# Three of four down units per MLP quarter computed with seven half-block products instead of eight

## The chip, the cores and the metric

The kernel runs on one core of a Trainium2 chip. The metric is the device time of one execution in microseconds, the median of 3 runs. Before the change these are 2278.57, 2278.39 and 2278.43 us.

## The reference, cut to what matters

Two decoder layers over 512 tokens of width 1024, all float32. Each has a token mixer (retention and stick-breaking attention, not touched by the change) and an MLP with a hidden width of 4096:

```python
h2 = _modulate(_rmsnorm(x, norm_mlp_g[l]), shift2, scale2)
u = jnp.square(jax.nn.relu(h2 @ w_up[l]))          # (512, 1024) @ (1024, 4096)
x = x + gate2[:, None, :] * (u @ w_down[l])        # (512, 4096) @ (4096, 1024)
```

## The kernel before

Activations lie transposed: channels in 128 partitions, 8 tiles of 128 channels (`k`), 512 tokens in the free dimension. To keep float32 accuracy each operand is split into a high part and a low part (`h_hi`, `h_lo`; `w_hi`, `w_lo`; `y_hi`, `y_lo` for u), and a product is three matmuls: high by high, high by low, low by high. Weights come in units of 256 output columns by 1024 rows: one 1 MB DMA into `w_raw` (two buffers, s = unit mod 2), ScalarE copies to `w_hi`, GpSimd subtracts to get `w_lo`. The DMA of a unit waits until GpSimd is done with the unit two before it. Each engine's program is written out by hand, in order, with semaphores between the engines; nothing is reordered.

The MLP runs in four quarters of the hidden width (f = 0 to 3). A quarter has eight units: 0 to 3 make 1024 channels of u (two tiles each), 4 to 7 multiply them by the down weights and add into x (`x_T`). In this text "unit 5" is the second down unit of a quarter.

A plain unit is `half_unit` twice: 8 tiles by 3 matmuls into one PSUM bank of 512 columns, so 48 matmuls of 512 columns. The up units of quarters 1 to 3 are made otherwise (`up_seven`): the unit is seen as a 2 by 2 block product (even and odd input tiles, first and second 128 output columns, first and second 256 tokens) and computed with seven half-block products instead of eight, a Winograd form. Each half-block product is 4 tiles by 3 matmuls of 256 columns: 84 matmuls of 256 columns for a unit. TensorE issues products one, five, four of the unit before, six, three, two, seven (L1513 is the matmul in `half_product`). The form needs sums of weight blocks (`sums_31`, `sums_24`: VectorE L2138, L2141, L2144 in `sum_weights`, then splits on ScalarE L586 to L593, low parts on GpSimd and on VectorE L2151) and sums of h blocks (t1 to t4: VectorE in `sum_h` and `sum_t`, once in each layer, in the down units of quarter 0). The extra copies of the weight sums, `wx_hi` and `wx_lo`, have two buffers. PSUM banks are joined by VectorE with the help of ScalarE copies (`first_copied`, `fifth_copied`, `sixth_copied`), since VectorE adds a PSUM bank and an SBUF copy of another. All products of ScalarE that TensorE waits for in a seven-product unit are in one in-order queue: high parts of the next unit's weights, the copies, the relu.

In quarter 0 the up units are plain: ScalarE takes the relu out of PSUM (L1014), VectorE squares (L2215), ScalarE makes `y_hi` (L1017), VectorE `y_lo` (L2218), for each of the eight tiles; then unit 4 waits for these tiles one after another (`u_split`). Unit m of a quarter sets its bank free with the relu.

Of the kernel before, what the change touches and what calls it, by code (L numbers as in the profile page):

```python
# [9 lines left out]
P = 128  # L10
D = 1024
SEQ = 512
# [74 lines left out]
FIRST_SEVEN = 1  # L87
SEVENS = 4 * (QUARTERS - FIRST_SEVEN)
PAIRS = KT // 2
T1, T2, T3, T4 = range(4)  # L90


def seven(layer, f, m):

    return SEVENS * layer + 4 * (f - FIRST_SEVEN) + m


def is_seven(unit):
    return unit >= MLP and (unit - MLP) % 8 < 4 and (unit - MLP) // 8 >= FIRST_SEVEN

# [36 lines left out]
def hybrid_trunk(nc, x, c, norm_mix_g, w_in, w_ret_out, w_sb_out, w_mix_out, norm_mlp_g,  # L137
# [7 lines left out]
    with ctx:  # L145
# [32 lines left out]
        wx_hi = nc.alloc_sbuf_tensor_at("wx_hi", [P, 2, 3, PAIRS, P], f32r, offset=work_base + 4 * 6144)  # L178
        wx_lo = nc.alloc_sbuf_tensor_at("wx_lo", [P, 2, 3, PAIRS, P], f32r, offset=ya_base)
# [68 lines left out]
        sums_31 = slab[:, 4 * PAIRS * HALF:4 * PAIRS * HALF + 2 * PAIRS * P].rearrange("p (a i n) -> p a i n", a=2, i=PAIRS)  # L248
        fifth = relu_t[:, 1, 0:HALF]
# [109 lines left out]
        h_summed, t_made, t_half, t_ready = sem("h_summed"), sem("t_made"), sem("t_half"), sem("t_ready")  # L359
# [98 lines left out]
        def _(pool):  # L458
# [23 lines left out]
            def seven_low(layer, unit):  # L482

                s, f, m = unit % 2, *divmod(unit - MLP, 8)
                q = seven(layer, f, m)
# [6 lines left out]
                for k in range(0, KT, 4):  # L492
                    ins = pool.tensor_tensor(w_lo[:, 2 * s + 1, k:k + 4:2, :], sums_31[:, 0, k // 2:k // 2 + 2, :],
                                             w_hi[:, 2 * s + 1, k:k + 4:2, :], ALU.subtract)
                ins.then_inc(seven_lo, 1)
                pool.wait_ge(seven_hi, 5 * q + 3)
                for i in range(0, PAIRS, 2):
                    ins = pool.tensor_tensor(wx_lo[:, s, 0, i:i + 2, :], sums_31[:, 1, i:i + 2, :],
                                             wx_hi[:, s, 0, i:i + 2, :], ALU.subtract)
                ins.then_inc(seven_lo, 1)  # L500
                pool.wait_ge(seven_hi, 5 * q + 5)
# [22 lines left out]
        def _(act):  # L524
# [51 lines left out]
            def seven_split(pair, unit, which):  # L576

                s, slot = unit % 2, 2 * (unit % 2)
                f, m = divmod((2 * pair + unit) % LAYER_UNITS - MLP, 8)
                q = seven((2 * pair + unit) // LAYER_UNITS, f, m)  # L580
                if which == 0:
                    act.wait_ge(raw_in[s], 16 * (pair + unit // 2 + 1))
                    ins = act.activation(w_hi[:, slot, :, :], w_raw[:, s, :, 0:P], ACT.Copy)  # L583
                elif which == 1:
                    act.wait_ge(sums_made, 3 * q + 1)
                    ins = act.activation(w_hi[:, slot + 1, 0:KT:2, :], sums_31[:, 0, :, :], ACT.Copy)  # L586
                elif which == 2:
# [141 lines left out]
            for layer in range(DEPTH):  # L729
# [1559 lines left out]
```

## Time and profile before

| | |
|---|---|
| median of 3 runs | 2278.43 us |
| profiled execution | 2278.35 us |
| its span (first to last instruction) | 2276.6 us |
| TensorE busy | 2256.1 us (99%) |
| VectorE, ScalarE, GpSimd busy | 1246.6, 976.2, 1228.2 us |
| granted TensorE clock, mean | 1.00 |

The chain that ended last is TensorE in 97% of the span. One MLP layer takes the stretch from about 806 to 1149 us in layer 0, and the same 1116.3 us later in layer 1. In a timeline row a first number is the start, the second how long the row's instructions took together; the bracket at the end is idle time of the engine before it and what ended it.

### The profile page before, as it was taken

The page shows a single profiled execution, that of the slowest core. Times are in us where ns is not written, and L with a number is a line of the kernel's source. Part 1 is how long each engine was busy: PE and PEld are TensorE (multiplying, and loading weights), DVE is VectorE, ACT ScalarE, POOL GpSimd, SP SyncE. Part 2 cuts the span into 40 slices and gives each one's busy share as a digit, 9 for nine tenths or more (in the row PEclk, how much of TensorE's full clock was granted, in tenths as well). Part 3 has the DMA queues.
Part 4 walks back from the last instruction along what each step waited for, and adds up shares of the span by engine and source line. Part 5 has one row for each costly group of instructions (what it writes and reads, how often), then busy time and mean ns, then how long its engine had stood idle before and what let it go on. Part 6 is the DMA issues. An engine that isn't in the chain of part 4 may idle for free.

```text
span 2276.6 us, 30866 instructions
## 1 busy us (share of the span) xinstructions
PE 2256.1 (99%) x12424; PEld 1921.7 (84%) x12424; DVE 1246.6 (55%) x1695; ACT 976.2 (43%) x1291; POOL 1228.2 (54%) x1538
## 2 busy tenths in 40 slices
PE   7999999999999999999999999999999999999998
PEld 5888888888888888998988888888888789898997
DVE  5776668546653346454476757441666524463453
ACT  4332233256675254453433323232666834353442
POOL 4454554544454457666555455455444444676663
PEclk9999999999999999999999999999999999999999
DMA  9445444422222222333334444222222222332332
GB/s 305 136 153 161 158 134 148 130 75 74 75 83 84 93 93 92 105 101 93 121 125 152 159 141 142 79 93 93 74 75 75 74 93 75 111 93 93 112 93 74
DMA packets 242094, 252.67 MB, mean 111 GB/s; under 512 B 3984, under 2 KB 237600, under 8 KB 241952
## 3 DMA queue, kind: packets, MB, share of 16 engines
q1 hardware_dynamic: 240272, 247.00, 33.6%
q10 hardware_dynamic: 1680, 3.70, 0.5%
q8 instruction: 98, 1.61, 0.3%
q14 instruction: 44, 0.36, 0.0%
HBM read 248.59 MB, written 2.10 MB: 110 GB/s over the span
## 4 chain that ended last, share of the span: by engine, by line
PE 97%; DVE 1%; ACT 1%; DMA 0%; issue 0%; SPq 0%; DVEq 0%; ACTq 0%
PE proj L1190 54%; PE att L1513 11%; PE proj L1213 6%; PE proj L1247 4%; PE proj L1230 4%; PE att L1230 4%; PE att L1403 2%; PE att L1453 2%; PE att L1278 2%; PE proj L1278 2%; PE att L1463 1%; PE att L1441 1%; PE att L1385 1%; PE proj L1352 1%; PE att L1416 1%; PE proj L1118 1%
## 5 line engine op out<-in xcount | busy, mean ns | idle before, releaser
L518 POOL TENSOR_TENSOR w_lo<-w_raw,w_hi 128x256 fp32r<-128x256 f32 x1280 | 1027.4, 836 | 934.7 <-ACT w_hi L564 797.1
L564 ACT ACTIVATE w_hi<-w_raw 128x1024 fp32r<-128x1024 f32 (+1 forms) x300 | 304.0, 1021 | 319.1 <-PE proj L1190 182.7
L1190 PE MATMUL proj<-h_hi,w_hi 128*128 128x512 f32 x1024 | 405.5, 396 | 0.0
L1190 PE MATMUL proj<-h_hi,w_lo 128*128 128x512 f32 x1024 | 399.3, 390 | 0.0
L1190 PE MATMUL proj<-h_lo,w_hi 128*128 128x512 f32 x1024 | 398.8, 389 | 0.0
L1190 PE MATMUL proj<-y_hi,w_hi 128*128 128x512 f32 x784 | 305.1, 389 | 0.0
L1190 PE MATMUL proj<-y_lo,w_hi 128*128 128x512 f32 x784 | 305.1, 389 | 0.0
L1190 PE MATMUL proj<-y_hi,w_lo 128*128 128x512 f32 x784 | 305.0, 389 | 0.0
L1190 PEld LDWEIGHTS proj<-h_hi,w_lo 128*128 128x128 f32 x1024 | 192.2, 188 | 41.2
L1190 PEld LDWEIGHTS proj<-h_hi,w_hi 128*128 128x128 f32 x1024 | 192.3, 188 | 40.4 <-issue 1.6
L1190 PEld LDWEIGHTS proj<-h_lo,w_hi 128*128 128x128 f32 x1024 | 192.6, 188 | 37.6
L1649 DVE SCALAR_TENSOR_TENSOR slab<-slab,c_act 128x256 f32<-128x256 f32 x280 | 177.0, 632 | 9.9
L1190 PEld LDWEIGHTS proj<-y_hi,w_lo 128*128 128x128 f32 x784 | 147.2, 188 | 30.7
L1190 PEld LDWEIGHTS proj<-y_hi,w_hi 128*128 128x128 f32 x784 | 147.2, 188 | 30.3
L1190 PEld LDWEIGHTS proj<-y_lo,w_hi 128*128 128x128 f32 x784 | 147.2, 188 | 29.9
L1767 DVE SCALAR_TENSOR_TENSOR x_T<-proj,mod,x_T 128x512 f32<-128x512 f32 x66 | 49.5, 750 | 196.1 <-PE proj L1190 196.1
L573 ACT ACTIVATE w_hi<-w_raw 128x512 fp32r<-128x512 f32 x64 | 37.0, 625 | 199.7 <-PE proj L1230 130.9
L488 POOL TENSOR_TENSOR w_lo<-w_raw,w_hi 128x256 fp32r<-128x256 f32 x96 | 90.3, 971 | 58.2 <-ACT w_hi L583 58.2
L2013 DVE TENSOR_TENSOR_SCAN slab<-slab,work 128x1280 f32<-128x1280 f32 x32 | 91.4, 2858 | 1.1
L2011 DVE SCALAR_TENSOR_TENSOR work<-att,work 128x1280 f32<-128x1280 f32 x32 | 47.6, 1487 | 60.9 <-ACT work L845 60.9
L2021 DVE TENSOR_TENSOR work<-att,slab 128x1280 f32<-128x1280 f32 x32 | 47.7, 1492 | 51.4 <-PE att L1453 51.4
L1247 PE MATMUL proj<-w_hi,h_hi 128*128 128x256 f32 x256 | 73.1, 286 | 0.0
(341 smaller groups left out, 4754.2 us busy)
## 6 DMA issues: line engine op xcount, KB each, us to landing
w_raw<-in_w_in SPq DMA_DIRECT2D x88, 1024.0 KB, 5.1
slab<-in_w_ada SPq DMA_DIRECT2D x42, 1024.0 KB, 6.3
w_raw<-in_w_up SPq DMA_DIRECT2D x32, 1024.0 KB, 5.6
w_raw<-in_w_down SPq DMA_DIRECT2D x32, 1024.0 KB, 5.2
w_raw<-in_w_ret_out SPq DMA_DIRECT2D x16, 1024.0 KB, 5.1
w_raw<-in_w_sb_out SPq DMA_DIRECT2D x8, 1024.0 KB, 5.1
w_raw<-in_w_mix_out SPq DMA_DIRECT2D x8, 1024.0 KB, 5.1
ya<-in_x SPq DMA_DIRECT2D x1, 2048.0 KB, 8.2
```

The source lines that it names most:

```text
L488: ins = pool.tensor_tensor(w_lo[:, 2 * s, k:k + 2, :], w_raw[:, s, k:k + 2, 0:P], w_hi[:, 2 * s, k:k + 2, :], ALU.subtract)
L518: ins = pool.tensor_tensor(w_lo[:, slot, k:k + 2, :], w_raw[:, s, k:k + 2, P * j:P * (j + 1)], w_hi[:, slot, k:k + 2, :], ALU.subtract)
L564: ins = act.activation(w_hi[:, 2 * s + j, ks, :], w_raw[:, s, ks, P * j:P * (j + 1)], ACT.Copy)
L1190: last = pe.matmul(proj[:, j, :], w[:, slot, k, :], a[:, k, :], start=k == 0 and n == 0, stop=k == KT - 1 and n == 2)
L1213: last = pe.matmul(first_bank if j == 0 and first_bank is not None else proj[:, j, :], w[:, slot, k, :], a[:, k, :], start=k == 0 and n == ...
L1230: last = pe.matmul(v_of(t).rearrange("p (a n) -> p a n", a=4), a[:, k, t * P:(t + 1) * P], w[:, :, k, :], start=k == 0 and n == 0, stop=k ...
L1247: last = pe.matmul(proj[:, t // 2, UNIT * (t % 2):UNIT * (t % 2 + 1)].rearrange("p (a n) -> p a n", a=2), a[:, k, t * P:(t + 1) * P], w[:, ...
L1278: last = pe.matmul(dst, w[:, slot, k, :], a[:, k, HALVES[t]], start=k == 0 and i == 0, stop=k == KT - 1 and i == 2)
L1513: last = pe.matmul(bank, w[b][at(i)], rows[a](i), start=begins and i == j == 0, stop=ends and i == PAIRS - 1 and j == 2, skip_group_check= ...
L1649: ins = dve.scalar_tensor_tensor(acc, raw[:, k, :], c_act[:, k:k + 1], acc, ALU.mult, ALU.add)
L1767: free(dve.scalar_tensor_tensor(x_T[:, k, :], proj[:, half, :], mod[:, ds(gate_col + k, 1)], x_T[:, k, :], ALU.mult, ALU.add), half)
L2013: own.link(dve.tensor_tensor_scan(logits[:, a, ::-1], carry_t[:, ::-1], terms[:, a, ::-1], 0.0, ALU.mult, ALU.add))
```

## The change

Units 5, 6 and 7 of quarters 0, 1 and 2 are made with seven half-block products too, in both layers: 18 units. Unit 4 of each quarter, and all down units of quarter 3, stay plain. What comes with it:

- Four sums of u blocks (`tu_sum`, `sum_tu`), made for each pair of tiles as soon as it is there: four VectorE instructions of 128x256 for each up unit of quarters 0 to 2. In quarters 1 and 2 ScalarE copies one half tile out of PSUM first (`b12_copied`). Then four splits of 128x1024 on ScalarE (`split_tu`) and four on VectorE (`low_tu`) for each quarter, in unit 4.
- The sums of h (`sum_t`) are no longer made from a float32 sum of h in `ya`, but from `h_hi` and `h_lo`: ten VectorE instructions of 128x1024 instead of eight. They stand in up units 1 and 2 of quarter 0 instead of down units 4 and 5.
- The weight sums take one buffer (`wx_hi`, `wx_lo` without the dimension of 2). One sum is made in place in `w_raw`, one in `decay_t`: four VectorE instructions of 128x512 instead of one of 128x1024 and two of 128x512. The split of sums two and four (`seven_split(..., 3)`) and `low_sums` wait until product three of the unit before is done.
- Down units made of seven products add to x from the joined banks (`add_tile`).

```diff
-FIRST_SEVEN = 1
-SEVENS = 4 * (QUARTERS - FIRST_SEVEN)
+DOWN = 4
+SEVEN_UNITS = ([8 * f + m for f in range(1, QUARTERS) for m in range(DOWN)]
+               + [8 * f + DOWN + d for f in range(QUARTERS - 1) for d in (1, 2, 3)])
...
-        wx_hi = nc.alloc_sbuf_tensor_at("wx_hi", [P, 2, 3, PAIRS, P], f32r, offset=work_base + 4 * 6144)
-        wx_lo = nc.alloc_sbuf_tensor_at("wx_lo", [P, 2, 3, PAIRS, P], f32r, offset=ya_base)
+        wx_hi, wx_lo = (nc.alloc_sbuf_tensor_at(name, [P, 3, PAIRS, P], f32r, offset=ya_base + 4 * 3 * PAIRS * P * i)
+                        for i, name in enumerate(("wx_hi", "wx_lo")))
...
```

ScalarE in each unit made of seven products (`ahead` splits the next unit's weights), then at the entry to the down units of quarters 0 to 2:

```diff
                     ahead(0)
+                    if after_up:
+                        high_u(f, 2 * j - 2)
                     act.wait_ge(made[1], q + 1)
                     act.activation(relu_t[:, 0, 0:HALF], chain_bank(q), ACT.Copy).then_inc(first_copied, 1)
                     ahead(1)
                     act.wait_ge(made[5], q + 1)
                     act.activation(fifth, FIFTH, ACT.Copy).then_inc(fifth_copied, 1)
                     ahead(2)
...
-                    ahead(3)
                     ahead(4)
...
+                    act.wait_ge(made[3], q + 1)
+                    ahead(3)
...
+                    for which in (1, 2, 4):
+                        seven_split(layer, f, DOWN + 1, which)
+                    split_tu(f, T1)
+                    split_tu(f, T2)
+                    seven_split(layer, f, DOWN + 1, 3)
+                    split_tu(f, T3)
+                    split_tu(f, T4)
...
```

TensorE's waits and products, the t sums of h on VectorE, and VectorE's down units:

```diff
+                    wait_t(f, j, T1)
                     pe.wait_ge(seven_lo, 3 * q + 3)
...
                     pe.wait_ge(fifth_copied, q + 1)
-                    half_product(3, wx, in_extra(s, 2), h_block(1, 1), FIFTH, False, True)
+                    half_product(3, wx, in_extra(2), block_of(up, 1, 1), FIFTH, False, True)
...
+                    if which in (T1, T3):
+                        b, a = ((b12, b11), (b22, b12))[which // 2]
+                        own.link(dve.tensor_tensor(t[which], b[0], a[0], ALU.subtract))
+                        own.link(dve.tensor_tensor(t[which], t[which], b[1], ALU.add))
+                        ins = dve.tensor_tensor(t[which], t[which], a[1], ALU.subtract)
...
+                def down(pair, f):
+                    if f > 0:
+                        square_first(f, 3)
+                        join_22(seven(layer, f, 3))
+                    sum_weights_13(f, DOWN + 1)
+                    if f > 0:
+                        first_of_u(f, 3)
+                        square_second(f, 3)
+                        second_of_u(f, 3)
+                    sum_weights_24(f, DOWN + 1)
+                    low_tu(f, T1)
+                    low_tu(f, T2)
+                    add_to_x(pair, MLP + DOWN, 0, 0, gates + KT * GATE2)
+                    low_sums(f, DOWN + 1)
+                    low_tu(f, T3)
+                    low_tu(f, T4)
+                    add_to_x(pair, MLP + DOWN, 1, 1, gates + KT * GATE2)
+                    for d in (1, 2, 3):
+                        seven_unit(f, DOWN + d)
```

VectorE's order in up units 1 and 2 of quarter 0. Before, from tile 2 on (L2215 squares a tile, L2218 makes its low part):

```order
L2215 TENSOR_TENSOR work<-work 128x512 [waits bank_free0]
L2218 TENSOR_TENSOR y_lo<-work,y_hi 128x512 [waits u_half]
L2215 TENSOR_TENSOR work<-work 128x512 [waits bank_free1]
L2218 TENSOR_TENSOR y_lo<-work,y_hi 128x512 [waits u_half]
L2215 TENSOR_TENSOR work<-work 128x512 [waits bank_free0]
L2218 TENSOR_TENSOR y_lo<-work,y_hi 128x512 [waits u_half]
```

The same place after the change (L2346 and L2350 square and make the low part, L2187 to L2189 and L2193, L2194 are t sums of h, L2249 sums of u):

```order
L2346 TENSOR_TENSOR work<-work 128x512 [waits tu_made,bank_free0]
L2350 TENSOR_TENSOR y_lo<-work,y_hi 128x512 [waits u_half]
L2187 TENSOR_TENSOR work<-h_hi 128x1024
L2188 TENSOR_TENSOR work<-work,h_lo 128x1024 [waits dve_own]
L2189 TENSOR_TENSOR work<-work,h_lo 128x1024 [waits dve_own]
L2346 TENSOR_TENSOR work<-work 128x512 [waits bank_free1]
L2350 TENSOR_TENSOR y_lo<-work,y_hi 128x512 [waits u_half]
L2249 TENSOR_TENSOR work<-work 128x256
L2249 TENSOR_TENSOR work<-work 128x256 [waits tu_made]
L2249 TENSOR_TENSOR work<-work 128x256
L2249 TENSOR_TENSOR ya<-work 128x256 [waits tu_made]
L2193 TENSOR_TENSOR work<-h_hi,work 128x1024 [waits t_made]
```

Two pairs of a square and its low part that followed each other now have up to seven instructions between them.

VectorE after the change in unit 4 of quarter 0, from the weight sums of unit 5 to the first weight sum of unit 6 (L2209, into `decay_t`); L2255 is `low_tu`, L1843 adds the halves of unit 4 to x, L2226 is `low_sums`:

```order
L2209 TENSOR_TENSOR decay_t<-w_raw 128x512 [waits raw_in1]
L2210 TENSOR_TENSOR w_raw<-w_raw 128x4x128
L2217 TENSOR_TENSOR att<-w_raw 128x512 [waits sums_made]
L2220 TENSOR_TENSOR att<-w_raw,att 128x512 [waits sums_made]
L2255 TENSOR_TENSOR tu_lo_63<-work,h_hi 128x1024 [waits tu_half]
L2255 TENSOR_TENSOR tu_lo_64<-work,h_lo 128x1024 [waits tu_half]
L1843 SCALAR_TENSOR_TENSOR x_T<-proj,mod,x_T 128x512 [waits proj_done]
L2226 TENSOR_TENSOR wx_lo<-att,wx_hi 128x1024 [waits seven_hi]
L2255 TENSOR_TENSOR tu_lo_65<-work,tu_hi_61 128x1024 [waits tu_half]
L2255 TENSOR_TENSOR tu_lo_66<-ya,tu_hi_62 128x1024 [waits tu_half]
L1843 SCALAR_TENSOR_TENSOR x_T<-proj,mod,x_T 128x512 [waits proj_done]
L2209 TENSOR_TENSOR decay_t<-w_raw 128x512 [waits seven_lo,raw_in0]
```

The first weight sum of unit 6 is the last of twelve.

ScalarE after the change from the entry of unit 5 in quarter 0 (L598: first high part of unit 6, L1002 copies product one, L601 splits the sum in `decay_t`, L1007 copies product five for the join):

```order
L598 ACTIVATE w_hi<-w_raw 128x1024 [waits raw_in0,proj_done]
L1002 ACTIVATE work<-att 128x256 [waits made1]
L601 ACTIVATE w_hi<-decay_t 128x4x128 [waits sums_made]
L1007 ACTIVATE ada_rows<-att 128x256 [waits made5]
L604 ACTIVATE wx_hi<-w_raw 128x512 [waits sums_made]
```

The copy of product five stands behind the split of that weight sum, here as in the up units before the change.

## Rows read from the trace of the kernel before

**Rows 1.** The page: busy time (share of span), and the chain that ended last by engine.

```profile
PE 2256.1 (99%) x12424; PEld 1921.7 (84%) x12424; DVE 1246.6 (55%) x1695; ACT 976.2 (43%) x1291; POOL 1228.2 (54%) x1538
...
PE 97%; DVE 1%; ACT 1%; DMA 0%; issue 0%; SPq 0%; DVEq 0%; ACTq 0%
```

**Rows 2.** The chain in order of time (start, us, what): layer 0, quarters 0 to 2.

```profile
820.54 76.19 PE proj L1190 x336
896.72 38.87 PE att L1513 x324
938.46 42.19 PE proj L1190 x186
980.65 38.87 PE att L1513 x324
```

**Rows 3.** Stretches of quarter 0's up units, then quarter 1's up and down units: busy time.

```profile
core 0: us, PE busy (x) PEld busy (x) DVE busy (x) ACT busy (x) POOL busy (x), PEclk, DMA share, GB/s
820.00:857.90 37.90, 37.90 (x171) 31.45 (x170) 12.48 (x16) 16.72 (x23) 22.77 (x31) 1.00 0.35 112
...
896.60:938.40 41.80, 41.80 (x344) 41.41 (x343) 27.16 (x39) 25.58 (x44) 30.91 (x39) 1.00 0.34 109
938.40:980.60 42.20, 42.20 (x188) 34.93 (x187) 10.81 (x13) 10.04 (x12) 24.55 (x34) 1.00 0.34 102
```

**Rows 4.** VectorE's timeline, quarter 0: tiles 1 to 4 (start us, us).

```profile
822.60 0.85 DVE L2215 TENSOR_TENSOR work<-work 128x512 f32<-128x512 f32 x1 [0.74 <-ACT work L1014]
824.14 1.15 DVE L2218 TENSOR_TENSOR y_lo<-work,y_hi 128x512 fp32r<-128x512 f32 x1 [0.70 <-ACT y_hi L1017]
826.67 1.15 DVE L2215 TENSOR_TENSOR work<-work 128x512 f32<-128x512 f32 x1 [1.38 <-ACT work L1014]
828.52 1.15 DVE L2218 TENSOR_TENSOR y_lo<-work,y_hi 128x512 fp32r<-128x512 f32 x1 [0.70 <-ACT y_hi L1017]
...
838.94 0.69 DVE L2218 TENSOR_TENSOR y_lo<-work,y_hi 128x512 fp32r<-128x512 f32 x1 [0.70 <-ACT y_hi L1017]
```

**Rows 5.** GpSimd's timeline, the same stretch.

```profile
822.16 6.97 POOL L518 TENSOR_TENSOR w_lo<-w_raw,w_hi 128x256 fp32r<-128x256 f32 x8 [2.63 <-ACT w_hi L564]
```

**Rows 6.** VectorE's timeline, unit 6 of quarter 0: t sums, alone and beside GpSimd.

```profile
870.23 1.22 DVE L2115 TENSOR_TENSOR work<-ya 128x1024 f32<-128x1024 f32 x1
871.48 1.64 DVE L2118 TENSOR_TENSOR work<-ya,work 128x1024 f32<-128x1024 f32 x1
```

**Rows 7.** GpSimd's timeline, the same stretch and the next: eight instructions of one form.

```profile
870.75 4.36 POOL L518 TENSOR_TENSOR w_lo<-w_raw,w_hi 128x256 fp32r<-128x256 f32 x4 [1.08 <-ACT w_hi L564]
...
881.95 2.83 POOL L488 TENSOR_TENSOR w_lo<-w_raw,w_hi 128x256 fp32r<-128x256 f32 x4
```

**Rows 8.** VectorE by line and shape: count, busy us, mean ns of one.

```profile
L2174 DVE TENSOR_TENSOR att<-work,att 128x256 f32<-128x256 f32 x24 | 10.1, 422 | 0.0
...
L1802 DVE TENSOR_TENSOR work<-work 128x256 f32<-128x256 f32 x18 | 8.4, 466 | 0.0
L2151 DVE TENSOR_TENSOR wx_lo<-att,wx_hi 128x1024 fp32r<-128x1024 f32 x6 | 7.4, 1226 | 8.1 <-ACT wx_hi L591 8.1
```

**Rows 9.** ScalarE by line and shape.

```profile
L983 ACT ACTIVATE work<-att 128x256 f32<-128x256 f32 x24 | 9.2, 384 | 8.8 <-PE att L1513 8.0
...
L943 ACT ACTIVATE t_hi<-work 128x1024 fp32r<-128x1024 f32 x8 | 8.0, 1044 | 0.0
```

**Rows 10.** VectorE's timeline, from the last up unit into unit 4 of quarter 1.

```profile
935.62 0.70 DVE L2162 TENSOR_TENSOR att<-work,att 128x512 f32<-128x512 f32 x1 [0.67 <-ACT work L997]
936.23 0.42 DVE L2174 TENSOR_TENSOR att<-work,att 128x256 f32<-128x256 f32 x1
...
939.13 0.70 DVE L2167 SCALAR_TENSOR_TENSOR att<-work,att 128x512 f32<-128x512 f32 x1 [1.46 <-ACT work L955]
940.49 0.69 DVE L2157 TENSOR_TENSOR y_lo<-att,y_hi 128x512 fp32r<-128x512 f32 x1 [0.67 <-ACT y_hi L949]
942.61 0.75 DVE L1767 SCALAR_TENSOR_TENSOR x_T<-proj,mod,x_T 128x512 f32<-128x512 f32 x1 [1.42 <-PE proj L1190]
```

**Rows 11.** ScalarE's timeline, first up unit of quarter 1.

```profile
898.19 0.38 ACT L978 ACTIVATE work<-att 128x256 f32<-128x256 f32 x1 [0.37 <-PE att L1513]
```

More of the change, by code:

```diff
@@ L482, in seven_low @@
             def seven_low(layer, unit):
[L484 to L485 removed]
+                s = unit % 2
+                q = seven(layer, *divmod(unit - MLP, 8))
+                second = raw_block(s)[:, A21, :, :]
                 pool.wait_ge(seven_hi, 5 * q + 1)
@@ L1017, in up @@
                             act.activation(y_hi[:, k, :], u_t[:, half, :], ACT.Copy).then_inc(u_half, 1)
-                            split_weights(pair, MLP + m + 2, half)
-                def down(pair, f, last):
-                    for m in range(4 if not last else 2 if layer < DEPTH - 1 else 3):
+                            if m < 3:
+                                split_weights(pair, MLP + m + 2, half)
+                            if m >= 2:
+                                split_t(2 * (m - 2) + half)
@@ new lines, in last_down @@
+                def last_down(pair, f):
+                    q = seven(layer, f, DOWN - 1)
+                    high_u(f, KT - 2)
+                    act.wait_ge(made[7], q + 1)
+                    split_weights(pair, MLP + DOWN + 1, 0)
+                    relu_second(q)
+                    high_u(f, KT - 1)
+                    split_weights(pair, MLP + DOWN + 1, 1)
+                    if layer < DEPTH - 1:
+                        products(pair, MLP + DOWN, 0)
+                        act.dma_start(rope_t, rope).then_inc(rope_in, 16)
+                    for m in range(2 if layer < DEPTH - 1 else 3):
@@ L2219, in quarter @@
                                               ALU.subtract).then_inc(u_split, 1)
-                    for m in range(4 if not last else 2 if layer < DEPTH - 1 else 3):
+                            if half == 1:
+                                for which in range(4):
+                                    sum_tu(0, m, which, u_t[:, 0, :], u_t[:, 1, :])
+                            if m in (1, 2):
+                                sum_t(2 * (m - 1) + half)
+                            elif k == 6:
+                                low_t(T1)
@@ L2225, in quarter @@
-                            add_to_x(pair, MLP + 4 + m, half, k, gates + KT * GATE2)
-                            if f == FIRST_SEVEN - 1:
-                                for i in ((0, 1), (2, 3))[half] if m == 0 else ():
-                                    sum_h(i)
-                                for which in ((T1, T2), (T3, T4))[half] if m == 1 else ():
-                                    sum_t(which)
-                            if not last and k == 3:
-                                sum_weights(pair + 4, f + 1, 0)
@@ L2233, in quarter @@
-                            if not last and k == 5:
-                                low_sums(f + 1, 0)
-                            if f == FIRST_SEVEN - 1 and k in (5, 6):
-                                for which in ((T1, T2), (T3, T4))[k - 5]:
-                                    low_t(which)
-                            if last and layer < DEPTH - 1:
+                            add_square(2 * layer + 2, k - 1, at_layer)
+                            add_to_x(pair, MLP + DOWN + m, half, k, gates + KT * GATE2)
```

441 lines of the change are left out of this document (266 added, 175 removed).

## The prediction

> **What bounds the kernel now.** I read the page's busy times and chain first: TensorE is busy for 99% of the span and is 97% of the chain that ended last [rows 1]. Only fewer or cheaper matmuls, or a wait of TensorE, can change the time. The chain in order of time then shows how tight this is in the stretch that changes: 336 plain matmuls in 76.19 us, 324 of the short ones in 38.87 us, and plain ones again, without a hole [rows 2]. The stretches show what the others have left: VectorE is busy for 12.48 of 37.9 us in the up units of quarter 0, for 27.16 of 41.8 us in up units of seven products, for 10.81 of 42.2 us in down units; GpSimd is at 22.77, 30.91 and 24.55 us [rows 3]. The timelines of single instructions come last, for the orders in which these two could become late.
>
> **The matmuls removed.** A plain one takes 76.19/336 = 226.8 ns, a unit of 48 takes 10.88 us. A short one takes 38.87/324 = 120.0 ns, a unit of 84 takes 10.08 us [rows 2]. Each converted unit saves 0.80 us, not an eighth of 10.88, because 256 columns cost more than half of 512. 18 units: 14.5 us less.
>
> The Trainium skill (TensorE: Matmul & The Clock Gate, "Back-to-back issue gap") gives columns/2.4 + 2.5 ns, which is 215.8 and 109.2 ns; as an estimate by that page a unit would save 1.19 us, 18 units 21.4 us. The rows have 226.8 and 120.0 ns, and the sum goes by them.
>
> **Quarter 0, up units: VectorE.** Unit 4 should start at 820.54 + 3 x 10.88 = 853.2 and asks for tile 7 of u 21 matmuls later, at 857.95. VectorE now does more between the tiles. After tile 1, ready at about 825.3 [rows 4], and until tile 7's low part is made it has: six tiles, each a square and a low part of 0.69 us with a gap of 0.70 us while ScalarE makes the high part [rows 4], 6 x 2.08 = 12.5 us; three sets of four sums of u, 0.42 to 0.47 us each [rows 8], less the 0.1 by which instructions without a wait overlap, 3 x 1.65 = 4.95; ten t sums of 1.22 us [rows 6], 12.1; one low part of t, 1.2. That is 30.7 us, so tile 7 is ready at 856.0, 1.9 us early. This is the lower bound, with no extra.
>
> The extra is in the rows. A VectorE instruction with two SBUF inputs that begins while GpSimd runs takes longer: 1.15 instead of 0.69 us [rows 4], 1.64 instead of 1.22 [rows 6], so 0.42 to 0.46 us for each, whatever its length. GpSimd loses time too: four instructions take 4.36 instead of 2.83 us beside two of 1.22 [rows 7], eight take 6.97 instead of 5.66 beside four of 0.69 [rows 5]. The Trainium skill (GPSIMD Engine Reference, "1. Specifications") states that GpSimd's SBUF interfaces are shared with VectorE and contended by VectorE instructions with two SBUF inputs. This speaks against the change, since nearly all that it adds in quarter 0 has two; the trace agrees with it: `low_sums` has a PSUM input and stays at 1.226 us [rows 8].
>
> In this stretch GpSimd has about 20 instructions, the rest of unit 2's low parts and those of units 3 and 4. Each can lengthen one VectorE instruction: at most 20 x 0.46 = 9.2 us. Six fall into VectorE's gaps, and some beside instructions that follow without a wait. I take 12, 5.5 us: tile 7 at 861.5, between 856.0 and 865.2. TensorE stands still for about 3.5 us.
>
> **Quarter 0, entry to unit 5.** In the new order the first weight sum of unit 6 is the last of twelve VectorE instructions, ScalarE's split of it stands ahead of the copy of product five, and product three needs that copy. Due for product three: 864.07 + 36 x 0.12 = 868.4. From tile 7's low part on VectorE has: sums of u 1.55, weight sums of unit 5 0.69 x 4 = 2.65, 0.65 of waiting for ScalarE's splits, two low parts 2.35, an add 0.65 (0.75 less the overlap) [rows 10], `low_sums` 1.2, two low parts 2.35, an add 0.7, the weight sum 0.65: 12.75. ScalarE's split and the copy of 0.384 [rows 9] add 1.05: 13.8 us. Queued behind the split on ScalarE is only that copy, and TensorE waits for it. Lower bound: 856.0 + 13.8 = 869.8, 1.4 us late. With four or five extras of 0.46, of which the wait for ScalarE swallows some, 15.4 us: 861.5 + 15.4 = 876.9, 8.5 us late. This contains the 3.5 us. Upper bound: 865.2 + 15.6 = 880.8, 12.4 us late. ScalarE's four new splits of 1.04 us [rows 9] lie beside this. Value taken: 8.5 for each layer, 17.0 us.
>
> **Quarters 1 and 2, up units.** Four sums of u with a PSUM input (0.42 us, no extra) and one copy of 0.38 us on ScalarE are added for each unit; weight sums cost 2.8 to 3.6 instead of 3.05 us. VectorE goes from 8.3 to between 9.7 and 10.6 us in a unit of 10.08 us. Only units 1 and 2 of a quarter carry all of it, so it falls behind by 1 us at most and recovers in unit 3. The tightest user is product four, which needs the join made 1.8 us after a unit's start and begins at 2.88. I take nothing; the other end is 0.3 us for a quarter.
>
> **Quarters 1 and 2, entry to unit 5.** The same twelve instructions. From the start of unit 4 (935.5 in quarter 1): the join ends at 1.15 and the second square starts at 3.65 as now, the gap behind it is 0.67 and the low part ends at 5.7 [rows 10]; three sums of u to 6.7, two weight sums to 8.1, the remaining seven instructions 2.35 + 0.65 + 1.2 + 2.35 + 0.65 + 0.65 = 7.85, and 0.45 for one extra: 16.4. Split and copy: 17.25. Product three is due at 12.32 + 4.32 = 16.64, since unit 4 with the guest product four takes 10.88 + 1.44. Late by 0.6 us, with three more extras 2.0; I take 1.4. Four such entries: 5.6 us. ScalarE's wait for the end of product one (0.37 us idle) is not on this path [rows 11].
>
> **At nothing.** The wait of the single buffer: after product three's end 2.9 us of other products are left in the unit and 4.3 more come before product six of the next, and a split of 1.04 and `low_sums` of 1.23 us [rows 8, 9] fit. If they didn't, product six would wait. `add_tile` replaces `add_to_x` one for one. GpSimd does ten instructions in a unit instead of a plain one's eight, 1.4 us more, and has 4 us free in it. The up units of quarter 3 change only names of buffers. The DMA of a unit is triggered by GpSimd's last low part, 9 us or more ahead of its use.
>
> **The sum.** -14.5 + 17.0 + 5.6 = +8.1 us. On the profiled execution's 2278.35 us (span 2276.6 and 1.75 around it, 0.08 under the median of the runs) that is 2286.5, and on the median's scale too.
>
> **Rivals.** First: VectorE and GpSimd rarely meet. The lower bounds then hold: -14.5 + 2 x 1.4 + 4 x 0.6 = -9.3, 2269.1 us. For it: GpSimd is idle for 40% of the up stretch [rows 3]. Against: its next work is started by ScalarE right behind the high part, when VectorE starts on the sums.
>
> Second, which also covers the change doing no more than its matmul count says: nothing waits, TensorE alone counts: 2263.9 us. For it: VectorE's total in a quarter stays under TensorE's. Against: the order of single instructions above.
>
> Third: GpSimd falls behind too. It is slowed 1.53 us by two instructions of 1.22 us [rows 7]; in unit 5 of quarter 0 it starts 5 us late and has the low parts of t and u beside it, so product five of units 5 and 6 waits for `seven_lo`. It decides when these low parts come over 2 us later than VectorE's chain above allows, and costs 2 us in each layer behind a quarter 0 at its upper bound: -14.5 + 2 x 14.4 + 4 x 2.0 = +22.3, 2300.7 us. For it: the rates in [rows 5, 7]. Against: a unit of seven products has over 3 us of slack on GpSimd in [rows 3].
>
> **Chances.** Forecast 0.55, first rival 0.15, second 0.13, third 0.15, others 0.02. What a measurement here can tell from no change is 0.2%, 4.6 us. The forecast's own range is 2278 to 2294; about a third of it lies under 2283. Faster: 0.13 and most of the first rival, 0.28. Same: 0.20. Slower: 0.52. The range of 8 in 10 takes the first rival and leaves out half of the second and half of the third: 2266 to 2297.
>
> **What would show it.** In the profile after: 120 ns for the down units' short matmuls; in quarter 0 a hole of TensorE inside the first half of unit 4, released by VectorE's L2350, and a second before product three of unit 5, released by ScalarE's copy L1007; in quarters 1 and 2 only the second, of 0.6 to 2 us. VectorE at its limit between 825 and 861 us, with t sums of 1.6 us. I am wrong if TensorE runs through these places, if holes come at other products (a release by GpSimd means the third rival), or if the short matmuls with `tu` operands take another time.

## The result, and the profile of the changed kernel

The changed kernel took 2307.65 us (median of 4 runs, 2306.34 to 2307.76) against 2278.41 us (2278.17 to 2278.57) for the kernel before, run beside it: a ratio of 1.0127, 95% interval 1.0110 to 1.0145. It is slower by 29.2 us. The forecast was 2286.5 us, range 2266 to 2297; the direction was right, the size was not. The profiled execution took 2307.67 us, with a span of 2305.8.

Its page, to be held against [rows 1]: busy time, and the chain that ended last by engine.

```profile
PE 2258.9 (98%) x13072; PEld 1952.0 (85%) x13072; DVE 1451.5 (63%) x1987; ACT 1057.2 (46%) x1439; POOL 1302.7 (56%) x1574
...
PE 89%; DVE 7%; ACT 2%; issue 1%; DMA 0%; SPq 0%; DVEq 0%; ACTq 0%
```

There are 648 matmuls more, as meant: 1512 of half the columns (18 x 84) stand in the place of 864. But VectorE is now 7% of the chain, and TensorE's busy time has risen by 2.8 us although it has less to do. The waits of TensorE, longest first (us in total, times, longest), name the places in the MLP; none of these rows stands in the profile before.

```profile
PE att L1556 <- ACT ada_rows L1007: 14.9, 6, 3.0
PE proj L1233 <- DVE y_lo L2350: 8.2, 4, 2.2
...
PE proj L1233 <- issue: 2.5, 2, 1.3
...
PE proj L1233 <- ACT work L1035: 0.8, 2, 0.4
```

The first row is the forecast's wait before product three of unit 5, the second its wait inside unit 4 of quarter 0. The other two stand at the start of unit 4 and one unit before it. The four rows make 26.4 us, and -14.5 + 26.4 is +11.9, not +29.2. The chain in order of time (start, us, what) shows where the others are. The first three rows are quarters 0 to 2 of layer 0, the last three those of layer 1:

```profile
880.98 67.69 PE att L1556 x540
...
967.67 66.56 PE att L1556 x540
...
1053.25 66.53 PE att L1556 x540
...
2013.71 66.39 PE att L1556 x540
...
2099.11 65.07 PE att L1556 x540
...
2183.19 66.55 PE att L1556 x540
```

All six rows are the same 540 short matmuls, without a wait, from product three of unit 5 to the end of the next up units. One takes 65.07 us, which is 120.5 ns each; the others take 1.3 to 2.6 us more, 8.4 us in all. The stretches behind the waits tell why (busy times by engine, then the granted clock in the third column from the end; first quarter 0 of layer 0, then quarters 1 and 2 of layer 1):

```profile
864.00:866.00 2.00, 1.47 (x4) 1.18 (x5) 1.97 (x6) 1.64 (x2) 0.28 (x1) 0.50 0.00 0
866.00:868.00 2.00, 2.00 (x6) 1.61 (x5) 2.00 (x2) 0.63 (x1) 2.00 (x3) 0.50 0.00 0
...
870.00:872.00 2.00, 2.00 (x10) 1.62 (x10) 1.71 (x3) 2.00 (x3) 2.00 (x2) 1.00 0.00 0
...
882.00:884.00 2.00, 2.00 (x11) 2.00 (x11) 1.97 (x3) 0.64 (x3) 2.00 (x3) 0.50 0.03 8
...
2098.00:2100.00 2.00, 0.89 (x7) 0.90 (x8) 1.97 (x3) 1.61 (x4) 1.85 (x3) 1.00 0.00 0
2100.00:2102.00 2.00, 2.00 (x19) 2.00 (x18) 1.11 (x2) 1.48 (x3) 2.00 (x3) 1.00 0.00 0
...
...
2185.00:2187.00 2.00, 2.00 (x11) 2.00 (x10) 0.23 (x1) 1.02 (x1) 2.00 (x4) 0.50 0.00 0
```

Behind a wait TensorE is busy all the time, but a row of 2 us counts 6 matmuls of 512 columns where the row at full clock counts 10, and 11 short ones where it counts 19. The granted clock is 0.50, its lower level of 1.2 GHz; before the change it was 1.00 in every stretch of [rows 3]. The starts of single matmuls give the price: 427 ns apart at 512 columns (866.40 and 866.83 below) instead of 226.8, 213 ns at 256 columns instead of 120.

```profile
861.40 0.50 PE L1233 MATMUL proj<-y_hi,w_hi 128*128 128x512 f32 x1 [1.92 <-DVE y_lo L2350]
...
864.53 0.80 PE L1233 MATMUL proj<-y_hi,w_hi 128*128 128x512 f32 x1 [2.15 <-DVE y_lo L2350]
...
866.40 0.63 PE L1233 MATMUL proj<-y_lo,w_hi 128*128 128x512 f32 x1
866.83 0.63 PE L1233 MATMUL proj<-y_hi,w_lo 128*128 128x512 f32 x1
...
880.98 0.58 PE L1556 MATMUL att<-y_hi,wx_hi 128*128 128x256 f32 x1 [3.01 <-ACT ada_rows L1007]
```

From 865.12 to 869.82 eleven matmuls lose 2.2 us in this way, and 2.4 us are lost at the same place of layer 1. With the 8.4 us above, TensorE loses 13.0 us at the low clock. That makes up the difference: measured from start to start, each of the 14 stops takes 0.2 to 0.5 us more than the idle time listed for it (the matmul at 864.53 is followed by the next one 0.59 us later), 4.2 us in all, and -14.5 + 26.4 + 13.0 + 4.2 = +29.1 us.

The Trainium skill (TensorE: Matmul & The Clock Gate, "What's actually happening") says that low is the clock's resting state and that activity of the engine releases it; the trace agrees as far as every slow stretch here follows a wait, but the equal wait at 2099.11 has none behind it.

Not all of the 13.0 us lengthen the kernel. VectorE works from tile 7 to the late weight sum without once waiting for TensorE, and product three comes 16.5 us after tile 7, whether unit 4 ran at the low clock or not (864.47 to 880.98 here; 858.05 to 874.57 in the experiment e7, where unit 4 ran at full clock). At full clock TensorE would only have waited longer before product three. So the 2.2 and 2.4 us inside unit 4 cost nothing in the end, and the 8.4 us behind product three do.

VectorE's timeline in the up units of quarter 0, against the 1.22 us of [rows 6] and the 0.69 of [rows 4] (start us, us):

```profile
846.26 1.22 DVE L2187 TENSOR_TENSOR work<-h_hi 128x1024 f32<-128x1024 f32 x1
847.51 1.64 DVE L2188 TENSOR_TENSOR work<-work,h_lo 128x1024 f32<-128x1024 f32 x1
...
850.75 1.22 DVE L2346 TENSOR_TENSOR work<-work 128x512 f32<-128x512 f32 x1
852.67 0.69 DVE L2350 TENSOR_TENSOR y_lo<-work,y_hi 128x512 fp32r<-128x512 f32 x1 [0.70 <-ACT y_hi L1038]
853.28 2.26 DVE L2249 TENSOR_TENSOR work<-work 128x256 f32<-128x256 f32 x3
855.46 0.95 DVE L2249 TENSOR_TENSOR ya<-work 128x256 f32<-128x256 f32 x1
...
863.78 0.69 DVE L2350 TENSOR_TENSOR y_lo<-work,y_hi 128x512 fp32r<-128x512 f32 x1 [0.70 <-ACT y_hi L1038]
```

While GpSimd runs (from 846.65 for 5.93 us, and from 853.67), one instruction after the other takes 0.42 to 0.54 us more: the square 1.22 instead of 0.69, a sum of u 0.95 (at 855.46) instead of 0.42. The first of the three sums in the row of 2.26 us began before GpSimd did and took 0.42 us, the other two took 0.94 us each. Tile 7's low part ends at 864.47. ScalarE's timeline shows a cost that the forecast had not seen:

```profile
852.01 0.63 ACT L1038 ACTIVATE y_hi<-work 128x512 fp32r<-128x512 f32 x1 [4.02 <-DVE work L2346]
852.55 1.04 ACT L580 ACTIVATE w_hi<-w_raw 128x1024 fp32r<-128x1024 f32 x1
853.50 1.04 ACT L959 ACTIVATE t_hi<-work 128x1024 fp32r<-128x1024 f32 x1
854.44 0.58 ACT L1035 ACTIVATE work<-proj 128x512 f32<-128x512 f32 x1
```

The relu L1035 empties the bank that TensorE needs for unit 4. It stands in ScalarE's queue behind two splits and behind L1038, which had waited 4.0 us for VectorE's square. It ends at 855.02, and unit 4 starts at 855.12, after 1.3 us without a releaser in the profile ("issue").

### The profile page after: what moved, and what is told of

The parts are those of the page before. It is cut to its first block, busy times and chain, and to the rows that moved or that the text cites. A ratio compares the mean times of both kernels' runs of the same rounds, so it can differ in the third digit from the quotient of the medians.

```text
span 2305.8 us, 32925 instructions
## 1 busy us (share of the span) xinstructions
PE 2258.9 (98%) x13072; PEld 1952.0 (85%) x13072; DVE 1451.5 (63%) x1987; ACT 1057.2 (46%) x1439; POOL 1302.7 (56%) x1574
## 4 chain that ended last, share of the span: by engine, by line
PE 89%; DVE 7%; ACT 2%; issue 1%; DMA 0%; SPq 0%; DVEq 0%; ACTq 0%
PE proj L1233 40%; PE att L1556 18%; PE proj L1256 5%; PE proj L1290 4%; PE att L1273 4%; PE proj L1273 4%; PE att L1446 2%; DVE tu_lo L2255 2%; PE att L1496 2%; PE att L1321 1%; PE proj L1321 1%; PE att L1506 1%; PE att L1484 1%; PE att L1428 1%; DVE work L2249 1%
## 5 line engine op out<-in xcount | busy, mean ns | idle before, releaser
L534 POOL TENSOR_TENSOR w_lo<-w_raw,w_hi 128x256 fp32r<-128x256 f32 x1136 | 921.3, 845 | 871.7 <-ACT w_hi L580 734.1
L580 ACT ACTIVATE w_hi<-w_raw 128x1024 fp32r<-128x1024 f32 (+1 forms) x264 | 265.9, 1016 | 228.7 <-PE proj L1233 103.9
L503 POOL TENSOR_TENSOR w_lo<-w_raw,w_hi 128x256 fp32r<-128x256 f32 x168 | 174.6, 1069 | 89.7 <-ACT w_hi L598 89.7
L1233 PE MATMUL proj<-y_hi,w_hi 128*128 128x512 f32 x496 | 196.0, 395 | 10.7 <-DVE y_lo L2350 8.2
L1233 PE MATMUL proj<-y_lo,w_hi 128*128 128x512 f32 x496 | 195.1, 393 | 0.0
L1233 PE MATMUL proj<-y_hi,w_lo 128*128 128x512 f32 x496 | 194.9, 393 | 0.0
L1233 PEld LDWEIGHTS proj<-y_hi,w_hi 128*128 128x128 f32 x496 | 94.5, 190 | 32.4 <-DVE y_lo L2350 9.9
L1233 PEld LDWEIGHTS proj<-y_hi,w_lo 128*128 128x128 f32 x496 | 94.3, 190 | 20.0
L1233 PEld LDWEIGHTS proj<-y_lo,w_hi 128*128 128x128 f32 x496 | 94.5, 190 | 19.2
L824 ACT ACTIVATE work<-proj 128x512 f32<-128x512 f32 x32 | 19.1, 598 | 122.4 <-PE proj L1233 122.4
```

Of the source, the lines that this page charges most:

```text
L503: ins = pool.tensor_tensor(w_lo[:, 2 * s, k:k + 2, :], w_raw[:, s, k:k + 2, 0:P], w_hi[:, 2 * s, k:k + 2, :], ALU.subtract)
L534: ins = pool.tensor_tensor(w_lo[:, slot, k:k + 2, :], w_raw[:, s, k:k + 2, P * j:P * (j + 1)], w_hi[:, slot, k:k + 2, :], ALU.subtract)
L580: ins = act.activation(w_hi[:, 2 * s + j, ks, :], w_raw[:, s, ks, P * j:P * (j + 1)], ACT.Copy)
L1233: last = pe.matmul(proj[:, j, :], w[:, slot, k, :], a[:, k, :], start=k == 0 and n == 0, stop=k == KT - 1 and n == 2)
```

## The experiments

**e3_holes: the price of a hole by itself.** The kernel before, with a wait of its own length in each quarter.

```
HOLE = (1, 2, 4, 5, 6, 7, 9, 14)
...
 products(pair, MLP + 4 + m, half)
+if m == 1 and half == 0:
+    for _ in range(HOLE[4 * layer + f]):
+        own.link(act.activation(hole_t[:, :], upto[:, :], ACT.Copy))
+    act.sem_inc(hole, 1)
...
+if m == half == 1:
+    pe.wait_ge(hole, 4 * layer + f + 1)
```

> The kernel before, with a hole made on purpose: in unit 5 of each quarter TensorE waits before its second half until ScalarE, released by the end of the first half, has done n small copies, n = 1, 2, 4, 5 in layer 0 and 6, 7, 9, 14 in layer 1. Estimate 0.35 us a copy and 0.35 for the way there and back: holes of 0.7, 1.05, 1.75, 2.1, 2.45, 2.8, 3.5 and 5.25 us, 19.6 us in all. Theory A (behind a hole of about 2 us or more the granted clock goes to 0.5 for some 5 us, which costs about 2.4 us more): 2278.4 + 19.6 + 4 or 5 x 2.4 = 2308 to 2310 us, and the short holes cost only themselves. Theory B (a hole costs itself alone): 2298 us.

Measured: 2304.28 us (2 runs), 25.9 more. The holes were 0.44, 0.79, 1.47, 1.81, 2.15, 2.49, 3.17 and 4.88 us long, 17.2 in all. Behind the three longest TensorE was slow, for 1.7, 1.7 and 2.2 us more than at full clock; behind the fifth it was not. Its stretches behind the fifth, and around the sixth:

```profile
1995.00:1997.00 2.00, 2.00 (x11) 1.63 (x10) 0.00 (x0) 0.00 (x0) 2.00 (x4) 1.00 0.68 239
2080.00:2082.00 2.00, 1.89 (x6) 1.52 (x7) 0.00 (x0) 1.07 (x2) 0.68 (x1) 0.69 0.57 201
2082.00:2084.00 2.00, 2.00 (x6) 1.55 (x5) 0.00 (x0) 0.00 (x0) 2.00 (x4) 0.50 0.00 0
2084.00:2086.00 2.00, 2.00 (x10) 1.65 (x9) 0.00 (x0) 0.00 (x0) 0.12 (x1) 0.96 0.04 8
```

Theory A holds with a smaller size than its 2308 to 2310: the holes were shorter than estimated, and only three slow stretches came. By theory B the holes as measured would give 2295.6 us. Without any part of the change, holes make the clock fall.

**e10_equal_holes: the same length eight times.** As e3, with `HOLE = (5,) * 8`.

> e3 with five small copies at all eight places: eight holes of 2.15 us, about the length of the waits of 2.21 us that were followed by the lower clock at three places of four. In e3 one of 2.15 us was not, one of 2.49 us was. Theory A (near this length it is open whether the clock falls, so the same wait costs 2.2 us or about 4): 2278.4 + 8 x 2.1 = 2295 us and 1.2 to 2.2 us more for each place where it falls, 2297 to 2308 us, with some places of each kind in the profile. Rival (there is a fixed length between 2.15 and 2.21 us): 2295 us and no lower clock.

Measured: 2299.41 us (2 runs), 21.0 more. The waits were 1.81 us (I had read 2.15 from e3's fifth hole; five copies are its fourth), 14.5 us in all. Behind three of the eight the clock fell, and 1.6 to 1.7 us were lost at each. Around the first and behind the third:

```profile
872.00:874.00 2.00, 2.00 (x6) 1.61 (x5) 0.88 (x1) 0.65 (x1) 1.27 (x2) 0.50 0.97 315
...
1047.00:1049.00 2.00, 2.00 (x10) 1.62 (x10) 0.00 (x0) 0.89 (x1) 1.03 (x2) 1.00 0.76 267
```

So the same wait after the same work costs 1.8 or 3.5 us, and the rival, a fixed length between 2.15 and 2.21 us, is gone: 1.81 can be enough, 2.21 can be too little.

**e2_filled: the holes before product three filled with matmuls.**

```
 pe.wait_ge(first_copied, q + 1)
+if j == DOWN + 1:
+    for _ in range(2):
+        repeated(6 if f == 0 else 5, wx, in_extra(1), t_block(up, T2), chain_bank(q))
 half_product(6, wx, in_extra(1), t_block(up, T2), chain_bank(q), False, False)
```

> Before product six of unit 5 TensorE repeats its matmuls into the same sum, 24 times in quarter 0 and 20 in quarters 1 and 2 (2.9 and 2.4 us at 120 ns), so the sum of that product is another one. TensorE is then busy where it stood still, and product three starts at the same time. Theory A (a hole makes the granted clock fall, and this costs about 12 us behind the six holes before product three): 2307.7 - 12 = 2295 us, between 2292 and 2299. Theory B (the low clock doesn't hang on the holes): 2307 to 2309 us.

Measured: 2299.80 us (4 runs), 7.9 less than the changed kernel, with 128 more matmuls. The waits before product three are 0.4 us in all, and no stretch behind them is slow. The filling costs 128 x 0.12 = 15.4 us and takes away 14.5 us of waiting, with 1.4 us of new waits, so 7.9 + 0.9 + 1.4 = 10.2 us of low clock came back: the 8.4 us of the chain's rows, and 1.6 us that the stretches behind unit 4 happened to be shorter. The 12 us of the expectation were too many; theory A holds, at 2300 instead of 2295 and just outside its 2292 to 2299.

**e1_copy_first: another order on ScalarE.**

```
-ahead(1)
+if j != DOWN + 1:
+    ahead(1)
 act.wait_ge(made[5], q + 1)
 ...
 act.activation(fifth, FIFTH, ACT.Copy).then_inc(fifth_copied, 1)
+if j == DOWN + 1:
+    ahead(1)
```

> In unit 5 of quarters 0 to 2 ScalarE copies product five before it splits the first weight sum of unit 6, so product three no longer waits for twelve VectorE instructions. Theory A (the loss is made of two things: holes of TensorE, 14.9 us of them before product three, and the stretch at the lower granted clock behind each of them, about 12 us in all): both go, 2307.7 - 14.9 - 12 = 2281 us, with the holes inside unit 4 of quarter 0 left (8.2 us and their low clock). Theory B (only waits cost; the lower clock comes with the change whatever waits there are): 2307.7 - 14.9 = 2293 us, with the low stretches still there. Theory C (VectorE is behind as a whole, so the wait only moves to the next product that needs it): 2300 us or more, with holes of the same sum before products six or one of unit 6.

Measured: 2294.63 us (2292.92 to 2297.27), ratio 1.0073 [1.0056, 1.0090]. The number is near theory B's, but B is wrong: in quarters 1 and 2 no stretch is slow any more. A is wrong too in its size, because half of the wait moved:

```profile
PE proj L1236 <- DVE y_lo L2353: 8.2, 4, 2.2
PE att L1559 <- ACT work L1020: 7.8, 6, 2.0
...
PE att L1559 <- POOL wx_lo L513: 2.0, 2, 1.2
```

ScalarE's copy for product seven (L1020) is now behind three splits of late sums. This is C's mechanism in part: the sums are late, and the order on ScalarE only decides who waits.

**e4_quarter0_plain and e5_plain0_copy: quarter 0 without the change.** e4 leaves the down units of quarter 0 plain and makes the t sums of h in them; e5 adds e1's edit.

```
-SEVEN_UNITS = (... + [8 * f + DOWN + d for f in range(QUARTERS - 1) for d in (1, 2, 3)])
+SEVEN_UNITS = (... + [8 * f + DOWN + d for f in range(1, QUARTERS - 1) for d in (1, 2, 3)])
```

> The down units of quarter 0 stay plain, as in the kernel before, and the sums of h are made in them (ten VectorE instructions); only those of quarters 1 and 2 are of seven products (12 units instead of 18). Theory A (each place pays for itself): saved 12 x 0.80 = 9.6 us; lost in each of four entries to unit 5 2.4 us of waiting and up to 2 us of low clock, 9.6 to 17.6 us: 2278.4 to 2286 us, and quarter 0 costs the changed kernel the other 21 to 29 us. Theory B (the loss comes from the new form of the unit wherever it stands): two thirds of the loss stay, 2297 us.

> Quarter 0 plain (as in e4) and the copy of product five ahead of the split (as in e1). In e1 the waits of 2.2 us in quarters 1 and 2 became waits of 1.1 us before product seven, released by ScalarE's copy L1020, which now stands behind three splits of sums that VectorE makes late; no lower clock showed behind them. Theory A (the late weight sums of unit 6 decide, the order on ScalarE only shifts who feels them): e4's 2283.0 - 4 x 1.1 of waiting - 5.3 of low clock = 2273.3 us, 2272 to 2275. Theory B (the lower clock comes with the change): 2278.5 us.

Measured: e4 2283.01 us (10 runs, 2278.74 to 2284.79), ratio 1.0018 [1.0008, 1.0027]; e5 2274.22 us (10 runs), ratio 0.9982 [0.9972, 0.9992]. So quarter 0 costs the changed kernel 24.6 us, net of what its six units save. In e4 each of the four entries waits 2.2 us, with the clock low behind three of them in the profiled execution; its runs lie up to 6 us apart, and their mean granted clock goes with it, from 0.999 in the two fastest to 0.996 or 0.997 in the others: how many waits are followed by the low clock differs. In e5 they are 1.1 us and nothing is slow. A's sum of 2273.3 holds.

**e6_sums_early and e11_sums_early_alone: the weight sums of unit 6 earlier on VectorE.** e6 is e5 with this edit, e11 is e4 with it.

```
 low_tu(f, T3)
+sum_weights_13(f, DOWN + 2)
+sum_weights_24(f, DOWN + 2)
 low_tu(f, T4)
 add_to_x(pair, MLP + DOWN, 1, 1, gates + KT * GATE2)
...
-if before_seven:
+if before_seven and j != DOWN + 1:
```

> As e5, and VectorE makes the four weight sums of unit 6 ahead of the fourth low part of the sums of u and of the second addition to x, instead of behind them: nothing that ScalarE's copies of unit 5 stand behind comes late any more. Theory A: no wait of TensorE over 0.3 us in the MLP, 2278.4 - 12 x 0.80 = 2268.8 us, with 0.3 us for each of the changes between plain and seven products 2268 to 2271. Rival C (VectorE is short of time, not badly ordered): the wait moves to product four or to product seven, which need the low parts T4 and T3: 2272 us or more.

> Quarter 0 plain, the weight sums of unit 6 made early, but ScalarE's copy of product five still behind the split (e6 without e1's edit). Theory A (lateness of the sums is the cause, and ScalarE's order hurts only when they are late): 2269 to 2270 us, as e6. Rival (the split itself, 0.6 us, stands in the way of the copy): a wait of 0.3 to 0.6 us before product three at four places, 2270.5 to 2272 us.

Measured: e6 2269.29 us (2269.12 to 2269.61), ratio 0.9960 [0.9944, 0.9976]; e11 2269.44 us, the same. They beat the kernel before by 9.1 and 9.0 us, of 12 x 0.80 = 9.6 possible. e6's chain in order of time, for quarter 0, the up units of quarter 1, unit 4, and units 5 to 7 with the next up units:

```profile
820.59 76.19 PE proj L1249 x336
896.77 38.89 PE att L1572 x324
938.61 9.55 PE proj L1249 x42
948.15 69.30 PE att L1572 x576
```

No hole is left, 69.30/576 is 120.3 ns, and the pair-by-pair sums, the single buffer and `add_tile` cost nothing that can be seen. VectorE is busy for 35.38 of 42 us from 948 to 990: it was not short of time there, it was badly ordered by 2.2 us. With the sums in time ScalarE's order doesn't matter.

**e9_all18_sums_early: the same order with all 18 units.** e1's edit and e6's on the changed kernel.

> All 18 down units of seven products, as in the changed kernel, with both edits of e6 (copy of product five first, weight sums of unit 6 ahead of the low part T4). Theory A: quarters 1 and 2 run without a wait; in quarter 0 the waits of unit 4 (4.1 us) and at its start (1.3 and 0.4 us) stay with about 2 us of low clock, and VectorE, about 8 us behind by then, makes TensorE wait 2 to 4 us more in unit 5 or 6. e6's 2269.3 - 6 x 0.80 + 2 x (5.8 + 2 + 2 to 4) = 2284 to 2288 us. Theory B (quarter 0 also heals by the order): 2278 us or less.

Measured: 2291.08 us, ratio 1.0056 [1.0041, 1.0071]. Quarters 1 and 2 run without a wait, as expected. Quarter 0 doesn't heal, and is worse than the 2284 to 2288 expected: beside unit 4's waits (8.1, 2.5 and 0.8 us) there are 5.5 us in three waits released by GpSimd's L513, at product five of units 5 and 6, and the clock is low behind three waits in the profiled execution (864.57, 1986.54 and 2008.06 us), but not behind the one of 2.30 us at 886.05.

```profile
PE proj L1236 <- DVE y_lo L2353: 8.1, 4, 2.2
...
PE att L1559 <- POOL wx_lo L513: 5.5, 3, 2.4
```

**e7_thin_gpsimd and e8_short_t: why VectorE is late in quarter 0.** e7 takes GpSimd's work away beside it, e8 six of the ten instructions of the t sums. Each leaves the rest of the changed kernel as it is.

```
e7: -for k in range(ks.start, ks.stop, 2):
    +for k in range(ks.start, ks.start + 2 if MLP + 2 <= unit <= MLP + 4 else ks.stop, 2):
e8: -own.link(dve.tensor_tensor(t[which], b[0], a[0], ALU.subtract))
    -own.link(dve.tensor_tensor(t[which], t[which], b[1], ALU.add))
    -ins = dve.tensor_tensor(t[which], t[which], a[1], ALU.subtract)
    +ins = dve.tensor_tensor(t[which], b[0], a[0], ALU.subtract)
    ...
```

> The changed kernel, where GpSimd makes only a quarter of the low parts (one instruction of four) for units 2, 3 and 4 of quarter 0, so that VectorE has it hardly beside it in the up units; the other low parts are left as they were, and the output is another one. Theory A (VectorE falls behind there because nearly each of its instructions with two SBUF inputs takes 0.42 to 0.54 us more beside GpSimd): tile 7's low part comes at 857 to 858 instead of 864.5 us, the waits of unit 4 and at its start (5.7 us a layer) shrink under 1.5, product three of unit 5 starts at about 874 instead of 881.0: 2307.7 - 2 x 7 - 2 x 2.3 of low clock = 2289 us. Theory B (VectorE has simply too many instructions, GpSimd matters little): 2303 us or more.

> The changed kernel with each of the four t sums made by a single VectorE instruction (the low terms of h left out; 4 instructions instead of 10 in each layer). It takes six instructions of 1.22 to 1.75 us, 9 us, from VectorE between tiles 1 and 7. Theory A: tile 7 comes at its time, the waits in unit 4 and at its start go, product three of unit 5 stays 4 to 6 us late, since the chain from tile 7 to it (16.5 us) stays: 2307.7 - 2 x 7.5 - 2 x 2.3 = 2288 us. Rival (the waits in unit 4 come from the sums of u or from ScalarE's order): 2300 us or more.

Measured: e7 2293.38 us, e8 2291.34 us; 2289 and 2288 were expected. In both the waits of unit 4 and at its start are gone. VectorE's timeline in e7, up to tile 7's low part, without an extra:

```profile
855.97 0.69 DVE L2346 TENSOR_TENSOR work<-work 128x512 f32<-128x512 f32 x1
857.36 0.69 DVE L2350 TENSOR_TENSOR y_lo<-work,y_hi 128x512 fp32r<-128x512 f32 x1 [0.70 <-ACT y_hi L1038]
```

Tile 7 is ready at 858.05 instead of 864.47 us, with the same VectorE instructions, and the quarter itself starts 0.9 us later in this execution (its first matmul at 821.27, not 820.36): 7.3 us are GpSimd's doing. Product three starts at 874.57 instead of 880.98, again 7.3 us earlier in its quarter. In front of it a new wait of 2.0 us stands in both layers at product five, in layer 0 released by GpSimd's L513: with VectorE in time for unit 4, GpSimd is late next. But this wait is not the 3 to 4 us by which both expectations missed, because the copy of product five (L1007) is still held up by the split of the late weight sum. ScalarE in e7:

```profile
873.62 0.63 ACT L601 ACTIVATE w_hi<-decay_t 128x512 fp32r<-128x512 f32 x1 [4.70 <-DVE decay_t L2209]
874.15 0.36 ACT L1007 ACTIVATE ada_rows<-att 128x256 f32<-128x256 f32 x1
```

What was wrong is the expectations' 2 x 2.3 us of low clock inside unit 4: those lie ahead of product three and shorten only the wait there. Without them e7's sum is 2307.7 - 2 x 7.3 = 2293.1 us, and 2293.4 was measured; e8, where product three moved by the same 7.3 us, lies 1.8 us lower, with runs from 2289.6 to 2293.2.

## Why the prediction was wrong

**The matmuls removed: right.** 0.80 us a unit; e6 has 9.1 of 12 x 0.80.

**Quarter 0, up units: right in place and cause, too small.** The chain without extras (30.7 us, tile 7 at 856.0) is confirmed by e7: 858.05, or 857.1 with the later start of that execution taken off, where a quarter of GpSimd's work is left. I then took 12 extras of 0.46. In the trace 19 instructions between tile 1 and tile 7 are longer, by 9.4 us in all, and tile 7 comes at 864.5, near the upper bound of 865.2. The step that failed is "some beside instructions that follow without a wait" as a ground to count fewer: instructions issued back to back pay the extra each, so one GpSimd instruction doesn't lengthen only one. The four sums behind tile 5 are an example: the first took 0.42 us, the other three 0.94 to 0.95 each. The Trainium skill (SBUF — State Buffer, "SBUF: two separate sides") calls the pair of ports an exclusive lock held for a whole instruction, which would let each of them wait anew; the equal size of the extras at 256 and 1024 elements agrees with it. The sharing goes both ways: beside VectorE GpSimd took 2.42 us for two instructions and 5.93 for four, against 2.83 for four in [rows 7].

**A queue that I did not follow.** I priced the wait for tile 7 (3.5 us) and not what stands behind ScalarE's high part: the relu that frees the bank. It makes 0.4 and 1.3 us more of waiting in each layer. Like the low clock inside unit 4 these lie ahead of product three, and only shorten the wait there.

**Quarter 0, entry to unit 5: right in place, order and releaser, too small.** Product three came at 880.98, not 876.9; due was 868.4. From tile 7 it took 16.5 us, not 15.4. It was 12.6 us late, not 8.5: 3.0 us of the difference come from tile 7, 1.1 us from the chain behind it. In two layers that is 8.2 us.

**Quarters 1 and 2, entry: right, too small.** VectorE's timeline in quarter 1, and ScalarE's beside it:

```profile
961.97 1.21 DVE L2255 TENSOR_TENSOR tu_lo<-work,tu_hi 128x1024 fp32r<-128x1024 f32 x1
963.11 1.76 DVE L2255 TENSOR_TENSOR tu_lo<-ya,tu_hi 128x1024 fp32r<-128x1024 f32 x1
964.79 0.74 DVE L1843 SCALAR_TENSOR_TENSOR x_T<-proj,mod,x_T 128x512 f32<-128x512 f32 x1
965.45 1.24 DVE L2209 TENSOR_TENSOR decay_t<-w_raw 128x512 f32<-128x512 f32 x1
```

```profile
966.72 0.63 ACT L601 ACTIVATE w_hi<-decay_t 128x512 fp32r<-128x512 f32 x1 [3.71 <-DVE decay_t L2209]
967.26 0.36 ACT L1007 ACTIVATE ada_rows<-att 128x256 f32<-128x256 f32 x1
```

I had one extra on this chain and allowed for three more; it has four or five. Product three is 2.4 us late (with a wait of 2.2), not 1.4, and outside my 0.6 to 2.0. In four entries that is 4.0 us.

**Quarters 1 and 2, up units, and what was costed at nothing: right.** There is no wait, though VectorE is busy for 38.21 of 43.4 us and its joins fall from a period of 10.08 to 10.6 us in units 1 and 2. e6 shows the rest.

**TensorE's clock: no term at all.** The sum prices each hole at its own length, and this step failed too. I had read a granted clock of 1.00 in every row of before and did not ask what holes, which the kernel before didn't have, would do to it. TensorE lost 13.0 us at the low clock, of which the 8.4 us behind product three lengthened the kernel.

With the measured sizes the sum is -14.5 + 2 x 12.6 + 4 x 2.4 + 8.4 = +28.7 us, against +29.2. The forecast's +8.1 missed by 21: 8.4 by the clock and 12.2 by lateness of VectorE, 8.2 in quarter 0 and 4.0 in quarters 1 and 2. Without the clock's part the time would be 2299.3 us, still above the range; with an error of the clock alone it would be 2294.9, inside it. The larger error is VectorE's lateness, and in it the count of extras. The third rival (2300.7) came nearer in time, but its mechanism was not at work: no wait in the changed kernel is released by GpSimd. Waits released by GpSimd appear when VectorE is less late: in e7 and e8, and, where ScalarE copies product five first, in e1 (2.0 us) and e9 (5.5 us).

## What to carry to other kernels

A change that lets a full TensorE stand still must be priced with its clock: here a wait of 1.8 to 3 us cost up to 2.6 us more, at some places and not at others, which also spreads the runs. Only low clock behind the last place where TensorE waits for a late chain counts; ahead of it, the wait absorbs it. When VectorE and GpSimd are both busy, count the extra for each VectorE instruction with two SBUF inputs that GpSimd's busy time covers, back to back or not, and follow every in-order queue behind the late one. Before giving up such a change, look at what stands ahead of the late instruction: with quarter 0 plain, moving four sums by two places made +4.6 into -9.0 us.

## What the runs showed of the hardware that I had not expected

- The granted clock fell to 0.50 behind single waits of 1.81 us (three of eight in e10), 2.21 us (three of four in the changed kernel, and again three of four in each of e4, e7 and e8) and 2.49 to 4.88 us (three of three in e3), and stayed at 1.00 behind 2.15 us in e3, behind 2.30 us in e9 and behind all waits up to 1.62 us.
- At the lower level the rows show 427 and 213 ns from matmul to matmul for 512 and 256 columns, against 226.8 and 120 ns: the short form loses less (a factor of 1.78 against 1.88).
- VectorE instructions with a PSUM input kept their time beside GpSimd, with all that was going on: `low_sums` 1.21 us, the sums of u with a PSUM input 0.41 us. With two SBUF inputs the same sums took 0.42 us alone and 0.94 to 0.96 beside GpSimd.
- Open is what decides, for waits of equal length, whether the clock falls; the work before and behind them was the same.
